# Three delta-rule inverses in one mixer: tile after tile, or two full tiles in step with the short one behind

## The reference, cut to what matters

```
def gdn_block(s_mat, inp):
    q, k, v, beta, g = inp
    gam = cumsum(g)
    dec_incl = exp(where(t >= s, gam[t] - gam[s], -inf))
    a_mat = beta * strict(dec_incl) * (k @ k.T)
    rhs = beta * (v - exp(gam) * (k @ s_mat))
    u = triangular_solve(a_mat + eye(l), rhs)            # unit lower triangle
    o = (q @ k.T * dec_incl) @ u + exp(gam) * (q @ s_mat)
    s_new = s_mat * exp(gam[-1]) + (k * exp(gam[-1] - gam)).T @ u
```

## Time and profile before

| | before |
|---|---|
| time, median of 3 runs | 1792.94 us (1789.94 to 1794.67) |
| the profiled execution's own time | 1792.5 us |
| span of its trace | 1790.7 us |
| PE busy | 1259.6 us (70%) |
| DVE busy | 451.6 us (25%) |
| ACT busy | 371.8 us (21%) |
| POOL busy | 65.7 us (4%) |
| bytes read from HBM | 468.28 MB |

### The profile page before, as it was taken

The page is one execution under the profiler, slowest core; times in us unless marked ns, Lnnn a source line. Parts: engine busy times, 40 slices in busy tenths (PEclk is TensorE's granted clock), DMA queues, the critical chain, the costliest instruction groups (busy, mean ns, idle before and its releaser), DMA issues.

```text
span 1790.7 us, 26729 instructions
## 1 busy us (share of the span) xinstructions
PE 1259.6 (70%) x12028; PEld 835.7 (47%) x12028; DVE 451.6 (25%) x819; ACT 371.8 (21%) x756; POOL 65.7 (4%) x69
## 2 busy tenths in 40 slices
PE   6999986787847566466655799888566655565664
PEld 5777766673334333233323477774343323332332
DVE  3446444321051111011101236811421101110111
ACT  3343131113102111111111222533111111111112
POOL 0000004200000000000000001100000000000000
PEclk9999986667959888788878899997678878787888
DMA  6233010005379999999999232031879999999993
GB/s 248 95 141 108 1 36 3 3 12 205 148 307 380 421 420 421 420 420 421 420 421 421 106 141 94 1 118 69 357 276 420 422 420 420 420 421 420 421 421 152
DMA packets 72540, 473.23 MB, mean 264 GB/s; under 512 B 5600, under 2 KB 15072, under 8 KB 53600
## 3 DMA queue, kind: packets, MB, share of 16 engines
q1 hardware_dynamic: 70112, 466.68, 64.1%
q0 software_dynamic: 2304, 4.72, 0.8%
HBM read 468.28 MB, written 6.77 MB: 265 GB/s over the span
## 4 chain that ended last, share of the span: by engine, by line
PE 36%; DMA 30%; DVE 6%; SPq 6%; issue 3%; ACT 2%; DVEq 0%; ACTq 0%; POOLq 0%
DMA arena<-in_wu 25%; PE ps L1908 9%; PE ps L1498 6%; SPq L411 6%; PE ps L1858 5%; PE ps L1937 4%; DMA arena<-in_wg 4%; DVE arena L900 2%; PE ps L1927 2%; DVE h L900 1%; PE ps L2014 1%; PE ps L1486 1%; DVE uT L900 1%; PE ps L1874 1%; PE ps L1863 1%
## 5 line engine op out<-in xcount | busy, mean ns | idle before, releaser
L1498 PE MATMUL ps<-uT,arena 128*128 128x288 f32 x1216 | 310.3, 416 | 0.8 <-DVE uT L900 0.8
L1908 PE MATMUL ps<-arena,xn 128*32 128x256 f32 x2048 | 164.5, 490 | 157.1 <-issue 117.3
L1498 PEld LDWEIGHTS ps<-uT,arena 128*128 128x128 f32 x1216 | 234.7, 195 | 67.6 <-issue 2.2
L1908 PE MATMUL ps<-arena,uT 128*32 128x256 f32 x2048 | 164.8, 490 | 121.2 <-issue 84.8
L900 DVE TENSOR_TENSOR uT<-uT,ps 64x256 f32<-64x256 f32 (+2 forms) x88 | 36.1, 421 | 761.1 <-ACT uT L806 683.0
L1908 PEld LDWEIGHTS ps<-arena,xn 128*32 128x32 f32 x2048 | 92.4, 140 | 231.7 <-issue 216.7
L1908 PEld LDWEIGHTS ps<-arena,uT 128*32 128x32 f32 x2048 | 91.5, 140 | 194.3 <-issue 178.3
L1927 PE MATMUL ps<-arena,uT 128*32 128x256 f32 x2048 | 125.1, 384 | 21.6 <-issue 18.2
L815 ACT ACTIVATE xn<-ps 32x256 f32<-32x256 f32 x256 | 96.0, 375 | 199.5 <-PE ps L1927 106.8
L806 ACT ACTIVATE uT<-ps 64x256 f32<-64x256 f32 x64 | 24.1, 376 | 494.0 <-PE ps L1908 494.0
L1937 PE MATMUL ps<-xn,uT 128*128 128x512 f32 (+1 forms) x192 | 92.9, 609 | 18.9 <-DVE h L900 15.6
(11 more groups left out here) (314 smaller groups left out, 1175.2 us busy)
## 6 DMA issues: line engine op xcount, KB each, us to landing
arena<-in_wg SPq DMA_DIRECT2D x64, 2048.0 KB, 34.3
arena<-in_wu SPq DMA_DIRECT2D x64, 2048.0 KB, 31.0
arena<-in_wd SPq DMA_DIRECT2D x64, 2048.0 KB, 34.7
arena<-in_wA SPq DMA_DIRECT2D x11, 2048.0 KB, 8.4
arena<-in_wC SPq DMA_DIRECT2D x8, 2048.0 KB, 9.2
arena<-in_w_out_ab SPq DMA_DIRECT2D x4, 2048.0 KB, 10.0
arena<-in_w_out_c SPq DMA_DIRECT2D x2, 2048.0 KB, 11.7
xn_rows<-xn SPq DMA_DIRECT2D x4, 512.0 KB, 15.3
```

The lines of the kernel that those rows point to most:

```text
L1498: m_ = MM(ps[:, banks[t % len(banks)], 0:TOK], ring[s][:, k, (t % 4) * P:(t % 4 + 1) * P], uT[:, k, :], start=(k == 0), stop=(k == KD - 1))
L1908: m_ = MM(ps[SLOTS * g:SLOTS * (g + 1), 2 + n % 2, 0:H2], x[:, k, SLOTS * q:SLOTS * (q + 1)], w[s][:, k, H2 * (g % 2):H2 * (g % 2 + 1)], s ...
```

## The change

Tiles 0 and 1 are both set up before either inverse begins, and their levels then alternate; tile 2's levels are put in behind (its level 0 with their level 3, its level 1 with their level 4, and so on). For this each tile has its own `gTc`, `gTTc`, `gPc`, `gDc`, `gB`, and tiles 0 and 1 their own `gT64` and `gP6`; tile 2 has its own `gDQK`, `gDKK`, `gQ` and decay vectors. Each tile's product and updates share one bank (bank i). All solves and outputs come after the inverses. The turning of the first SSD state comes ahead of the GDN setup, that of the second behind tile 0's keys. The gate's SiLU on ACT is put between tile 0's exponentials and its values; the gate's multiplication on DVE between level 3 and level 4, its squares on ACT behind it, the sums on PE between `gdn_known(2)` and `gdn_output(1)`, and both scalings on DVE at the very end, ahead of `head_norm`. On POOL both tiles' masks, far blocks and tile 2's masks come ahead of `gdn_blocks(0)`.

```diff
+INVERSE = [(0, 0), (1, 0), (0, 1), (1, 1), (0, 2), (1, 2), (2, 0), (0, 3), (1, 3), (0, 4), (1, 4), (2, 1), (0, 5), (1, 5),
+           (2, 2), (0, 6), (1, 6), (2, 3), (2, 4)]
+PRODUCTS = [step for step in INVERSE if step[1]]
...
+        def inv_bank(i):
+
+            return bank(i, 2 * 8, SUB)
+
...
+        gTc, gTTc, gPc, gDc = [[compact[i][q] for i in range(TILES)] for q in range(4)]
...
             gdn_masked(0)
             gdn_far(0)
             gdn_sides(0)
-            gdn_blocks(0)
             gdn_masked(1)
             gdn_far(1)
+            gdn_masked(2)
+            gdn_blocks(0)
+            gdn_blocks(1)
             gdn_sides(1)
-            gdn_blocks(1)
-            gdn_masked(2)
             gdn_sides(2)
...
             gdn_setup(0)
+            gdn_setup2(0)
+            gates(0)
+            gdn_values(0)
+            gdn_setup(1)
+            gdn_setup2(1)
+            gdn_values(1)
...
+            act.wait_ge(S["yg_ready"], 1)
+            nc.scalar.activation(Z[:, 0:8, :], cat[:, 0:8, :], ACT.Square).then_inc(S["sq2_done"], 1)
+            gdn_p(0, 4)
...
+            ssd_final(0)
             gdn_decay(0)
+            ssd_final(1)
             gdn_mats(0)
             gdn_scores(0)
+            gdn_decay(1)
             gdn_level(0, 0)
+            gdn_mats(1)
+            gdn_scores(1)
+            gdn_level(1, 0)
             gdn_level(0, 1)
+            gdn_level(1, 1)
+            gdn_decay(2)
             gdn_level(0, 2)
...
             gdn_level(1, 2)
...
             gdn_mats(2)
             gdn_scores(2)
+            gdn_level(2, 0)
+            gdn_level(0, 3)
+            gdn_level(1, 3)
+            ssd_gate()
+            gdn_level(0, 4)
+            gdn_level(1, 4)
+            gdn_level(2, 1)
...
             gdn_solved(2)
             gdn_state(2)
+            ssd_scale()
...
+            ssd_turn(0)
             gdn_decays(0)
             gdn_keys(0)
+            ssd_turn(1)
+            gdn_values(0)
+            gdn_decays(1)
+            gdn_keys(1)
+            gdn_values(1)
+            gdn_first(0)
+            gdn_first(1)
+            gdn_product(0, 1)
+            gdn_product(1, 1)
+            gdn_decays(2)
+            gdn_update(0, 1)
+            gdn_update(1, 1)
+            gdn_product(0, 2)
+            gdn_product(1, 2)
+            gdn_keys(2)
+            gdn_update(0, 2)
+            gdn_update(1, 2)
+            gdn_first(2)
...
+            gdn_product(2, 4)
+            gdn_solve(0)
+            gdn_update(2, 4)
+            gdn_output(0)
+            gdn_known(1)
+            gdn_values(2)
+            gdn_solve(1)
+            gdn_known(2)
             pe.wait_ge(S["sq2_done"], 3)
...
-                    m_ = MM(ps[:, g, 0:TOK], ones, uT[:, 4 * g + c, :], start=(c == 0), stop=(c == 3))
+                    m_ = MM(ps[:, g, 0:TOK], ones, Z[:, 4 * g + c, :], start=(c == 0), stop=(c == 3))
...
             gdn_output(1)
...
             gdn_solve(2)
             gdn_output(2)
```

More of the change, by code:

```diff
@@ L178, in build @@
         gU = take(cur, STAGE, 8, P)
+        cur = [STAGE]
+        SSD_DEAD = RING + XBC_TILES * XW
+        gB = [None, take(cur, SSD_DEAD, INNER, 8, SUB), take(cur, SSD_DEAD, INNER, 8, SUB)]
+        compact = [None, [take(cur, SSD_DEAD, 8, SUB) for _ in range(4)], None]
+        for three in (gDQK, gDKK):
+            three.append(take(cur, SSD_DEAD, 8, SUB))
+        gQ2 = take(cur, SSD_DEAD, 8, SUB)
         cur = [in_pad]
@@ L705, in _, with gates, gdn_setup2 @@
                 z_evac(Z_AFTER[u])
[L706 to L710, removed]
+            def gates(g):
+                act.wait_ge(S["proj_evac"], CONV_TILES + Z_TILES)
+                nc.scalar.activation(Z[:, 8 * g:8 * g + 8, :], Z[:, 8 * g:8 * g + 8, :], ACT.Silu).then_inc(S["z_act"], 1)
             def gdn_setup(i):
-                L, s = LEN[i], i % 2
+                L = LEN[i]
                 GB = bank(3, 8, P, n=2)
                 act.wait_ge(S["gdn_gb"], i + 1)
[L716 to L720, removed]
+                nc.scalar.activation(gQ[i][:, :, 0:L], GB[:, :, 0:L], ACT.Exp)
+                nc.scalar.activation(gDec[i], GB[:, :, L - 1], ACT.Exp)
+                nc.scalar.activation(gEcum[i][0:L], cum[0:L, i, SSD_HEADS:SCAL], ACT.Exp).then_inc(S["gdn_exp"], 1)
+            def gdn_setup2(i):
+                L = LEN[i]
                 act.wait_ge(S["gdn_diff"], 2 * i + 1)
@@ L723, in gdn_setup @@
                 act.wait_ge(S["gdn_diff"], 2 * i + 2)
-                nc.scalar.activation(gTail[s][0:L], gTail[s][0:L], ACT.Exp).then_inc(S["gdn_exp"], 1)
+                nc.scalar.activation(gTail[i][0:L], gTail[i][0:L], ACT.Exp).then_inc(S["gdn_exp"], 1)
             def gdn_values(i):
@@ L752, in _ @@
             gdn_setup(0)
+            gdn_setup2(0)
[4 more added lines that the diff above has]
+            gdn_values(1)
+            gdn_p(0, 1)
+            gdn_p(1, 1)
+            gdn_setup(2)
+            gdn_p(0, 2)
+            gdn_p(1, 2)
+            gdn_setup2(2)
+            gdn_p(0, 3)
+            gdn_p(1, 3)
+            act.wait_ge(S["yg_ready"], 1)
+            nc.scalar.activation(Z[:, 0:8, :], cat[:, 0:8, :], ACT.Square).then_inc(S["sq2_done"], 1)
+            gdn_p(0, 4)
+            gdn_p(1, 4)
+            gdn_p(2, 1)
+            gdn_p(0, 5)
+            gdn_p(1, 5)
+            gdn_p(2, 2)
+            gdn_p(0, 6)
+            gdn_p(1, 6)
+            gdn_p(2, 3)
+            gdn_p(2, 4)
+            gdn_out(0)
+            gdn_values(2)
             act.wait_ge(S["nrm_ps"], 3)
@@ L1759, in gdn_output @@
                 m_.then_inc(S["gdn_o"], 1)
+            ssd_turn(0)
             gdn_decays(0)
             gdn_keys(0)
+            ssd_turn(1)
[16 more added lines that the diff above has]
+            gdn_first(2)
+            gdn_product(0, 3)
+            gdn_product(1, 3)
+            gdn_update(0, 3)
+            gdn_update(1, 3)
+            gdn_product(0, 4)
+            gdn_product(1, 4)
+            gdn_product(2, 1)
+            gdn_update(0, 4)
+            gdn_update(1, 4)
+            gdn_update(2, 1)
+            gdn_product(0, 5)
+            gdn_product(1, 5)
+            gdn_product(2, 2)
+            gdn_update(0, 5)
+            gdn_update(1, 5)
+            gdn_update(2, 2)
+            gdn_product(0, 6)
+            gdn_product(1, 6)
+            gdn_product(2, 3)
+            gdn_update(0, 6)
+            gdn_update(1, 6)
+            gdn_update(2, 3)
+            gdn_product(2, 4)
[3 more added lines that the diff above has]
+            gdn_known(1)
+            gdn_values(2)
+            gdn_solve(1)
+            gdn_known(2)
             pe.wait_ge(S["sq2_done"], 3)
```

313 lines of the change are left out of this document (115 added, 198 removed).

## The result

The changed kernel takes 1788.31 us (median, 1784.9 to 1792.99), the one before 1794.63 beside it: a ratio of 0.9963 with an interval of 0.995 to 0.9976. It is faster, by 6.3 us, where 15.3 were forecast; the time lies 0.3 us above the range. The profiled execution took 1787.26, its span 1785.4.

What follows compares the result with a forecast made beforehand. PE's pauses inside one tile's chain and half-clock matmuls were taken as the losses. Setup to 280, levels to 329, tail to 389, projection at 401.8 instead of 417.1: 15.3 us less than 1792.5, so 1777; range 1769 to 1784.

Steps and rivals of the forecast that it cites:

- Setup: Before the levels: setting up both tiles first delays PE's first product to about 280, losing 11 us.
- The levels in step ... so a round of both is PE's own time: Alternating levels of tiles 0 and 1: each tile fills the other's waits; sum 48.9 us, done at 329.
- rounds 1 to 4: First four alternating rounds of tiles 0 and 1, with tile 2's part: 8.6, 6.4, 9.6 and 11.3 us.
- the named pauses: PE pauses near 3 us at the first matmul of `gdn_first(2)`, and again at `gdn_update(0, 4)`, released by ACT.
- Levels 5 and 6: Last levels of tiles 0 and 1 with two tile 2 rounds: 13 us, allowing for savings at full clock.
- Less: the queues bind: Levels: stalls in longer 32x32 runs and queue neighbours lose 6 to 11 us; 1783 to 1788, chance 0.14.
- No change: Whole kernel: setup and tail cost what levels save, under 13 of 28 us; within 0.3%, chance 0.07.
- Slower: half clock end to end: PE at half clock throughout: levels 8.5 and tail 16.8 us more, 25.3 in all; 1802, chance 0.05.
- Tail: Solves, outputs and states in one chain after the levels: 57 us, plus 3 for stalls, ending at 389.
- PE at full clock through the tail: Rival: fewer pauses raise PE's clock, giving back 13 us plus 7; 1757, half of it 1767; chance 0.16.
- Seam: Last state to projection: two scalings (5.1 us) delay the weights' load, PE starts 7.7 later, at 401.8.
- after 417.1 nothing is edited: Behind the stage, from the landing of the output projection's first weights at 417.1: the change edits nothing there.

Runs made afterwards that it cites:

- half_updates: Changed kernel with one of the two halves of the update's product left out in levels 1 to 4; first product to tile 0's solve 51.0 us.
- dense_runs: Changed kernel plus 256 waitless 32x32 matmuls by 32 columns, then 128 by 128 columns, behind the last output; 1806.43 us, once.
- the three moves: Changed kernel with SiLU ahead of tile 0's exponents, gate multiplication behind tile 0's scores, scalings ahead of the last state; all together 1786.44 us, ratio 0.9956.
- after_again: The changed kernel run and profiled once more, unchanged; 1787.85 us, ratio 0.9964 to the kernel before.
- before_again: The kernel before the change, unchanged, run for a second profile; 1794.41 us.
- scale_hidden: Changed kernel with the two scalings on DVE moved ahead of the last state; 1786.78 us, ratio 0.9964 to the kernel before.
- tile_by_tile: Changed kernel's matrices, banks and setup, but levels run tile by tile again; 1795.19 us, ratio 1.0003 to the kernel before.
- staggered_plus: Changed kernel with tile 1 two levels behind tile 0, SiLU ahead of tile 0's exponents, scalings behind the last solved values; 1772.0 us, ratio 0.9888.
- staggered: Changed kernel reordered: tile 1 two levels behind tile 0, tile 0's solve and output among tile 1's levels 5 and 6; 1777.45 us, ratio 0.9917.
- gates_early: Changed kernel with ACT running the gate's SiLU ahead of tile 0's decay exponents; 1785.12 us, ratio 0.9954 to the kernel before.

## Why the prediction was right and wrong

- **Setup: right.** First product at 278.8 for 280. The last wait is the one forecast, for POOL's mask of tile 1 behind DVE's matrices (5.79 us).
- **"The levels in step ... so a round of both is PE's own time": this is the step that failed.** Forecast 48.9, measured 63.0. In rounds 1 to 4, mis-sized by 11.8 us, a round of two tiles has 384 records: three pieces, 10.4 us of supply, whatever PE's own time is, with tile 2's part and the named pauses on top (11.1 to 12.6 measured). `half_updates` and `dense_runs` show it. The 1.05 us stall in the earlier trace rows looks like the same mechanism: an instruction packet passed at 315.1 to 315.4, 2.6 to 2.9 us ahead of its end, as with the others. I had put 3 us for such stalls over the whole stage. Before, a tile's level had 192 records, 5.2 us of supply, in 5.6 to 10.4 us, and the supply kept up but for 3.5 us of issue stalls in the inverses of tiles 0 and 1. Levels 5 and 6, 15.4 for 13, are another matter: few instructions, PE busy 14.59 of 15.35 at half clock. There my assumption of a better clock failed: the gaps had closed, and the clock stayed at 0.50.
- **The rivals.** "Less: the queues bind" had the right place (32x32 runs with stalls); 1788 was its end. That the total came out so near was luck: the levels lost 14.1 us, not 6 to 11, and the tail gave some back. Its other reason, neighbours in the lists, was not borne out by the three moves (1.9 us together for 10.1). "No change" was nearer than its chance: it wanted the levels to save under 13 of 28 us, and they saved 14. "Slower: half clock end to end" was right on the clock in the levels (0.50 to 0.58); what it cost there next to the supply was not told apart, save in levels 5 and 6. In the tail it did not hold.
- **Tail: 53.1 for 57, and for 60 with the 3 for stalls**, at a granted 0.79. Known 1, solve 1, known 2 and solve 2 took 1.9 to 2.05 us each where I had 3.0 to 3.6: for them "PE at full clock through the tail" held, while output 2 took 12.79 at half clock as forecast. So errors of both signs make up the 6.3 us by which the projection came late: about 14 in the levels and 0.4 at the seam, less 1.2 in the setup, 4 in the tail and the 3 for stalls. The tail varies by 2 us: output 0 took 3.84 in this profile and 5.37 in `after_again`.
- **Seam: 13.2 for 12.8.** That the load would then wait for the store, had the scalings been hidden, I had the rows for.
- **Behind the stage: "after 417.1 nothing is edited" was taken for "nothing changes".** The router's matmuls answer to PE's clock, as these windows show, first `before_again`, from its router's start:

```profile
495.10:501.10 6.00, 6.00 (x46) 5.92 (x46) 0.41 (x2) 0.00 (x0) 0.00 (x0) 0.66 0.98 391
501.10:504.10 3.00, 0.42 (x7) 0.27 (x5) 2.13 (x15) 0.00 (x0) 0.00 (x0) 0.50 1.01 320
```

then `after_again`, likewise:

```profile
488.30:494.30 6.00, 6.00 (x30) 6.00 (x29) 0.29 (x1) 0.00 (x0) 0.00 (x0) 0.50 0.97 373
494.30:497.30 3.00, 2.09 (x21) 1.87 (x20) 0.69 (x5) 0.00 (x0) 0.00 (x0) 0.50 1.01 326
```

  Both profiles of before have the higher clock and 461.7 and 461.5 us from the router to the load of `wC`, both of the changed kernel 0.50 and 463.8 and 464.0. So 2.4 us are given back. Another part, up to 3.5 us, is scatter: from that load to the HGRN state's it took 220.5 and 220.7 in the first profile of before and in `scale_hidden`, and 223.7 to 225.4 in all others, 224.0 in the second profile of before. 9.0 - 2.4 = 6.6 us, against 6.3 in the medians; but the stage too has its scatter, 163.5 us in `after_again`, 168.7 in `before_again`, and with the means of both profiles the same sum is 7.1 - 2.4 = 4.7. What decides the clock there stays open. It is not how soon the stage ends: the router had 0.50 in `tile_by_tile` behind a stage of 172.0 us, and 0.68 in `staggered_plus` behind one of 146.9.

## What to carry to other kernels

Count PE's records, not only its time: on many small float32 matmuls the instructions themselves have a rate (here 128 records with their weight loads in 3.47 us, slower beside a large transfer), and putting two such chains in step helps only down to that rate. Where waits are put down to "issue" once in every 128 records, leave instructions out, or lay the dense stretches beside steps of few, long instructions, as the staggered order did: 16 us less than before, 22 with two of the small moves added, where the change alone had 6. Look at the unchanged stages too: part of a gain can go there, here 2.4 us to the clock of the router's matmuls. And before a small difference between two profiles is given a cause, profile the same kernel twice.

## What the runs showed of the hardware

- PE's instructions are fetched by the DMA engines, one packet of 16 KB for some 128 matmul records and 128 weight loads: in the stalled rounds of the levels one in 3.47 us, 4.00 beside 98 GB/s, 5.65 to 6.47 beside 296 to 413 GB/s.
- A granted clock of 0.50 to 0.58 stood over rounds where PE's records, nearly all 32x32 matmuls, covered 55 to 85% of the time, and 0.50 over 13.45 us of `staggered` that they covered wholly; 96 records of 128x128 matmuls among them brought it to 0.85 and more.
- VectorE lost time beside GpSimd: the multiplication of 128x1024 by the triangle took 3.20 us in `staggered_plus` and 2.91 in `gates_early` beside GpSimd's 128x1024 multiplication, and 1.22 in the changed kernel, where it stood alone. In `gates_early` this ate most of what the earlier SiLU had won.
